# Two-block transformer kernel on one core: four TensorE products left out at the head of each of three attentions

## The chip, the cores and the metric

The kernel runs on one core of a Trainium2 chip. The metric is the device time of one execution, in microseconds (us); smaller is better. Three runs of the kernel before took 2171.41, 2173.5 and 2172.23 us.

## The reference

Two transformer blocks run one after the other over 512 tokens of width 1024, all in float32. What matters here are their three softmax attentions of 8 heads. Cut to what is computed:

```python
def first_block(x, ...):
    # o_a: 8 heads of 64; keys chosen by an index score, plus a relative bias
    logits = jnp.einsum('bqhd,bqkhd->bhqk', qb, k_sel) * A_HEAD_DIM ** -0.5 + bias   # dim 64
    p = jax.nn.softmax(jnp.where(valid, logits, -jnp.inf))
    o_a = jnp.einsum('bhqk,bqkhd->bqhd', p, v_sel)
    x = x + jnp.concatenate([o_a, o_b], axis=-1) @ w_out     # o_b: gated linear attention
    return x + hier_moe(rmsnorm(x, norm2_g), ...)            # 32 experts

def hybrid_mixer(h, ...):
    o_mla = causal_block_attention(q_mla, k_mla, v_mla, 1 / sqrt(96))                # dim 96
    o_fox = causal_block_attention(fq, fk, fv, 1 / sqrt(64), cum_log_f)              # dim 64 + 2
    merged = sigmoid(gate_a) * (o_mla @ w_o_mla) + sigmoid(gate_b) * (o_fox @ w_o_fox)
    return merged @ w_out

def second_block(x, ...):
    x = x + gate_m * hybrid_mixer(rms_norm(x) * (1 + scale_m) + shift_m, ...)
    x = x + gate_f * moe_ffn(...)                            # 64 experts and a shared one
    return rms_norm(x, g_final)
```

## The kernel before

The program is a list of stages (L2423 to L2426): setup, first norm, mixers, first attention, first output, first experts; then the second norm, latents, latent attention, fox attention, merge, second experts, final norm. Each stage is made of one or more blocks. In a block, each engine has its own list of instructions with waits on semaphores written out by hand, and a block ends with a barrier that all engines pass together. A stage's loads are issued by SyncE inside its own blocks, and many of them wait for a count of products of TensorE.

The function `attention` (L902) is called three times: by `first_attention` (L1023, query and key of 64 rows, two heads packed on the upper and lower 64 rows, with a bias that GpSimd prepares at L1017 for up to six units ahead, and with rows of the other mixer gated on GpSimd between them at L1033 and L1036), by `latent_attention` (L2040, 96 rows) and by `fox_attention` (L2102, 66 rows). It works through 32 units, 8 heads times 4 tiles of 128 queries. Unit t of a head covers 128 (t + 1) keys. TensorE takes turns between the scores of unit i (L934: 64, 96 or 66 rows, 128 to 512 columns, bank i % 3), the transposes of the probabilities of unit i - 3 (L943: 128 rows, 128 columns, t + 1 of them, banks 3 and 4) and the output products of unit i - 5 (L953: 128 rows, 64 columns, t + 1 of them, banks 5 and 6). VectorE adds the mask or bias and takes the maximum (L990), negates it (L993), inverts the sum (L998) and scales the output (L1000). ScalarE takes the exponential (L972) and copies the transposes (L966).

At the head of TensorE's list stand four products (L926, L927; WARM_UP is 4 at L32): the identity times the causal mask, 128 rows, 512 columns, into bank 7. Attention writes banks 0 to 6 only, nothing waits for the four or reads bank 7, and they wait for nothing but the barrier.

What stands around the attentions: the mixers stage ahead of the first one ends with small products of TensorE (L579, L590) and work of VectorE and ScalarE (L740 to L827). `heads_to_columns` (L2008, transposes at L2021) stands ahead of the second and third. Behind the first come `turn_rows` (L1125: 32 transposes at L1138) and `add_rows_product` (L1163). Elsewhere the text speaks of these lines: L487 is the product of a helper in the mixers (the index scores on 32 rows among them, L487 also the projections on 128 rows), L507 and L508 are products with one output column, L339 are the transposes of a norm, L1360 is the router's product with 64 columns.

Of the kernel before, what the change touches and what calls it, by code (L numbers as in the profile page):

```python
# [28 lines left out]
TAKEN = -float(2 ** 120)  # L29
SENTINEL = float(2 ** 100)  # L30
NO_TOKEN = 4096
WARM_UP = 4  # L32
HEADS = 8
FE = 256
FH = 2
# [197 lines left out]
def product(K, mm):  # L233

    mm.then_inc(K.products, 1)
    K.n_products += 1
    return K.n_products
# [664 lines left out]
def attention(K, tag, dim, out_col, bias=None, keep=None, loads=(), heads=None, rest=None):  # L902

    nc = K.nc
    s = K.sem
    maxed, expd, turned = s(f"{tag}_max_ready"), s(f"{tag}_probs_ready"), s(f"{tag}_turned_copied")
    scored, normed = s(f"{tag}_logits_read"), s(f"{tag}_out_normed")  # L910
    query, key = heads or (lambda h: K.qt[0:dim, h, :], lambda h: K.kt[0:dim, h, :])
    z = K.scr[:, 3072:4608].rearrange("p (b s) -> p b s", b=3)
    RING = 6
    offsets = K.scr[:, 0:512 * RING].rearrange("p (b s) -> p b s", b=RING)
    offset_ready = s(f"{tag}_offsets_ready")
    probs = K.scr[:, 8192:10240].rearrange("p (b s) -> p b s", b=4)
    turn = K.scr[:, 4608:6144].rearrange("p (b s) -> p b s", b=3)
    mx, neg, rsum, rinv = (K.small[:, 576 + 32 * n:608 + 32 * n] for n in range(4))
    units = [(h, t) for h in range(HEADS) for t in range(T)]
    N = len(units)  # L920
    at_s, at_t, at_o = [], [], []
    with nc.Block(no_gpsimd_drain=True) as block:
        @block.tensor
        def _(pe):

            for _ in range(WARM_UP):  # L926
                pe.matmul(K.bank[7][:, :], K.ident[:, :], K.causal[:, :], start=True, stop=True)  # L927
            for i in range(N + 5):
                if i < N:
                    h, t = units[i]  # L930
                    n = P * (t + 1)
                    if i >= 3:
                        pe.wait_ge(scored, i - 2)
                    at_s.append(product(K, pe.matmul(K.bank[i % 3][:, 0:n], query(h)[:, P * t:P * t + P],  # L934
                                                     key(h)[:, 0:n], start=True, stop=True)))
                if 3 <= i < N + 3:
                    u = i - 3
                    h, t = units[u]
                    pe.wait_ge(expd, u + 1)
                    if u >= 2:  # L940
                        pe.wait_ge(turned, u - 1)
                    for k in range(t + 1):
                        mm = pe.transpose(K.bank[3 + u % 2][:, P * k:P * k + P], probs[:, u % 4, P * k:P * k + P],  # L943
                                          K.ident[:, :])
                    at_t.append(product(K, mm))
                if i >= 5:
                    u = i - 5
                    h, t = units[u]
                    pe.wait_ge(turned, u + 1)
                    if u >= 2:  # L950
                        pe.wait_ge(normed, u - 1)
                    for k in range(t + 1):
                        mm = pe.matmul(K.bank[5 + u % 2][:, 0:64], turn[:, u % 3, P * k:P * k + P],  # L953
                                       K.v[:, k, 64 * h:64 * h + 64], start=k == 0, stop=k == t)
                    at_o.append(product(K, mm))

        @block.scalar
        def _(act):
            for i in range(N + 3):
                if i >= 3:  # L960
                    u = i - 3
                    n = P * (units[u][1] + 1)
                    act.wait_ge(K.products, at_t[u])
                    if u >= 3:
                        act.wait_ge(K.products, at_o[u - 3])
                    act.activation(turn[:, u % 3, 0:n], K.bank[3 + u % 2][:, 0:n], ACT.Copy).then_inc(turned, 1)  # L966
                if i < N:
                    n = P * (units[i][1] + 1)
                    act.wait_ge(maxed, i + 1)
                    if i >= 4:  # L970
                        act.wait_ge(K.products, at_t[i - 4])
                    act.activation(probs[:, i % 4, 0:n], z[:, i % 3, 0:n], ACT.Exp, bias=neg[:, i:i + 1],  # L972
                                   accum_out=rsum[:, i:i + 1]).then_inc(expd, 1)

        @block.vector
        def _(dve):
            step = K.dve.on(dve)
            for i in range(N + 5):
                if i < N:
                    h, t = units[i]  # L980
                    n = P * (t + 1)
                    dve.wait_ge(K.products, at_s[i])
                    if i >= 3:
                        dve.wait_ge(expd, i - 2)
                    zi, logits = z[:, i % 3, 0:n], K.bank[i % 3][:, 0:n]
                    mask = K.causal[:, S - n:S]
                    if bias is not None:
                        dve.wait_ge(offset_ready, i + 1)
                        mask = offsets[:, i % RING, 0:n]
                    dve.tensor_tensor_reduce(zi, logits, mask, 1.0, float(MASKED) * 2, ALU.add, ALU.max,  # L990
                                             mx[:, i:i + 1]).then_inc(scored, 1)
                    dve.wait_ge(scored, i + 1)
                    dve.tensor_scalar(neg[:, i:i + 1], mx[:, i:i + 1], -1.0, None, ALU.mult).then_inc(maxed, 1)  # L993
                if i >= 5:
                    u = i - 5
                    h, t = units[u]
                    dve.wait_ge(expd, u + 1)
                    step(dve.reciprocal(rinv[:, u:u + 1], rsum[:, u:u + 1]))  # L998
                    dve.wait_ge(K.products, at_o[u])
                    dve.tensor_scalar(K.hr[:, t, out_col + 64 * h:out_col + 64 * h + 64], K.bank[5 + u % 2][:, 0:64],  # L1000
                                      rinv[:, u:u + 1], None, ALU.mult).then_inc(normed, 1)

        @block.sync
        def _(sp):
            for place, src, arrived in loads:
                sp.dma_start(place, src).then_inc(arrived, 16)

        @block.gpsimd
        def _(pool):
            if bias is None:  # L1010
                return
            pool.wait_ge(K.bias_in, 32)
            for i, (h, t) in enumerate(units):
                n = P * (t + 1)
                if i >= RING:
                    pool.wait_ge(scored, i - RING + 1)
                pool.tensor_tensor(offsets[:, i % RING, 0:n], bias(h)[:, S - n:S], keep[:, t, 0:n],  # L1017
                                   ALU.add).then_inc(offset_ready, 1)
                if rest and i % 4 == 3:
                    rest(pool, i // 4)  # L1020
# [1434 lines left out]
```

## Time and profile before

| what | us |
| --- | --- |
| median of three runs | 2172.23 |
| the profiled execution's own time | 2176.87 |
| its span, first to last instruction | 2175.1 |
| TensorE busy with matmuls | 1940.5 |
| VectorE busy | 1203.3 |
| ScalarE busy | 952.8 |
| GpSimd busy | 589.4 |

### The profile page before, as it was taken

Reading aid. Unit: us, or ns where it says so; the run is one execution under the profiler, and the core shown is the slowest. Engines: PE = TensorE matmul, PEld = TensorE weight load, DVE = VectorE, ACT = ScalarE, POOL = GpSimd, SP = SyncE. Lnnn points to the kernel's source line nnn. Section 1 sums busy time; section 2 is a strip of 40 time slices with the busy share of each in tenths; the row PEclk is TensorE's granted clock in tenths of the full one; section 3 lists DMA queues with packets and bytes.
Section 4 is the critical chain, followed back from the end, with each engine's and each line's share of the span. In section 5 each row is a group of like instructions: output and inputs, shape, how many; then the busy total and the mean of one; then the engine's idle time right before and its main releaser. Section 6 shows DMA issues by size and latency. Waiting matters only on the chain. (4 is left out here: it accounts for less than half of the span.)

```text
span 2175.1 us, 27110 instructions
## 1 busy us (share of the span) xinstructions
PE 1940.5 (89%) x8280; PEld 1332.8 (61%) x8280; DVE 1203.3 (55%) x2222; ACT 952.8 (44%) x1620; POOL 589.4 (27%) x435
## 2 busy tenths in 40 slices
PE   7989989976999997689998988979999999999992
PEld 3533435765777665367876876647766666666661
DVE  1755413526777774246164344447777777777663
ACT  2411214523666553356264222146655555555551
POOL 4799995101222222000000000012222222222221
PEclk9799989986999999789999999789999999999996
DMA  5353422351999994211202335229999999999983
GB/s 176 114 184 117 163 77 72 135 195 54 336 334 325 327 324 135 89 49 40 78 6 78 108 115 218 83 94 344 338 338 327 324 331 337 322 337 326 317 280 98
DMA packets 120530, 437.44 MB, mean 201 GB/s; under 512 B 31920, under 2 KB 36416, under 8 KB 83328
## 3 DMA queue, kind: packets, MB, share of 16 engines
q1 hardware_dynamic: 92760, 402.69, 50.2%
q0 software_dynamic: 27648, 33.67, 7.0%
q8 instruction: 45, 0.74, 0.1%
q14 instruction: 37, 0.30, 0.0%
q10 hardware_dynamic: 40, 0.05, 0.0%
HBM read 442.51 MB, written 63.48 MB: 233 GB/s over the span
## 5 line engine op out<-in xcount | busy, mean ns | idle before, releaser
L1528 DVE TENSOR_TENSOR big_parts<-big,h_cols_parts 128x1024 fp32r<-128x1024 f32 x384 | 460.1, 1222 | 126.9 <-ACT h_cols_parts L1581 118.4
L1581 ACT ACTIVATE h_cols_parts<-big 128x1024 fp32r<-128x1024 f32 x384 | 395.7, 1057 | 99.9 <-PE bank L1489 64.8
L1518 PE MATMUL bank<-big,heads 128*128 128x512 f32 x768 | 352.7, 602 | 1.5 <-ACT heads L1589 1.5
L1792 POOL DMA_INDIRECT acc_scratch<-heads,small x96 | 159.5, 1662 | 618.0 <-DVE small L1559 386.3
L1487 PE MATMUL bank<-h_cols_parts,heads_parts 128*128 128x512 f32 x768 | 312.7, 407 | 15.9 <-DVE heads_parts L1549 15.7
L1489 PE MATMUL bank<-h_cols_parts,heads_parts 128*128 128x512 f32 x768 | 304.0, 396 | 0.0
L1488 PE MATMUL bank<-big_parts,heads_parts 128*128 128x512 f32 x768 | 302.7, 394 | 0.0
L1518 PEld LDWEIGHTS bank<-big,heads 128*128 128x128 f32 x768 | 138.3, 190 | 139.8 <-issue 137.8
L1614 ACT ACTIVATE heads<-bank 128x512 f32<-128x512 f32 x96 | 57.4, 598 | 335.4 <-DMA acc_scratch<-heads,small 262.9
L1619 POOL MEMSET heads<- 128x2048 f32 x2 | 3.6, 1805 | 687.2 <-POOLq L1354 687.2
L1487 PEld LDWEIGHTS bank<-h_cols_parts,heads_parts 128*128 128x128 f32 x768 | 147.3, 192 | 47.7 <-DVE heads_parts L1549 11.3
L1489 PEld LDWEIGHTS bank<-h_cols_parts,heads_parts 128*128 128x128 f32 x768 | 146.2, 190 | 32.2
L1488 PEld LDWEIGHTS bank<-big_parts,heads_parts 128*128 128x128 f32 x768 | 146.9, 191 | 28.2
L487 PE MATMUL bank<-big,h_cols 128*128 128x512 f32 (+1 forms) x384 | 163.0, 580 | 0.0
L1631 POOL DMA_INDIRECT heads<-h_scratch,small x96 | 114.2, 1190 | 168.5 <-DVE small L1559 139.6
L1101 PE MATMUL bank<-big_parts,heads_parts 128*128 128x512 f32 x352 | 139.8, 397 | 0.0
L487 PEld LDWEIGHTS bank<-big,h_cols 128*128 128x128 f32 x384 | 73.2, 210 | 89.1 <-issue 88.5
L1549 DVE TENSOR_TENSOR heads_parts<-bank,heads_parts 128x512 fp32r<-128x512 f32 x192 | 123.1, 681 | 2.6 <-ACT heads_parts L1607 2.6
L1498 PE MATMUL bank<-ident,heads 128*128 128x128 f32 x768 | 105.8, 282 | 19.6 <-DMA heads<-h_scratch,small 19.0
L1498 PEld LDWEIGHTS bank<-ident,heads 128*128 128x128 f32 x768 | 98.8, 192 | 37.8 <-DMA heads<-h_scratch,small 32.7
L1607 ACT ACTIVATE heads_parts<-bank 128x512 fp32r<-128x512 f32 x192 | 103.7, 596 | 9.3 <-PE bank L1498 9.3
L1557 DVE TENSOR_SCALAR small<-bank 128x1 int32<-128x1 f32 x96 | 21.1, 219 | 141.9 <-DMA acc_scratch<-heads,small 140.3
(361 smaller groups left out, 3014.4 us busy)
## 6 DMA issues: line engine op xcount, KB each, us to landing
big<-in_w_exp_down_dram SPq DMA_DIRECT2D x96, 1024.0 KB, 14.2
big<-in_w_exp_gate_dram SPq DMA_DIRECT2D x96, 1024.0 KB, 7.1
big<-in_w_exp_up_dram SPq DMA_DIRECT2D x96, 1024.0 KB, 14.7
big<-in_w_in_dram SPq DMA_DIRECT2D x13, 2048.0 KB, 8.9
junk<-in_w_mod_dram SPq DMA_DIRECT2D x12, 1024.0 KB, 5.1
spare<-in_w_mod_dram SPq DMA_DIRECT2D x12, 1024.0 KB, 5.1
big<-in_w_out_dram SPq DMA_DIRECT2D x4, 2048.0 KB, 10.4
h_scratch<-h_rows SPq DMA_DIRECT2D x8, 512.0 KB, 7.6
```

What stands on the lines that cost most here:

```text
L487: mm = pe.matmul(out, lhsT, rhs, start=c == 0, stop=c == len(lhs_rhs) - 1)
L1101: pe.matmul(banks[t][:, :], a_high, low, start=False, stop=False)
L1487: pe.matmul(b_au[b][:, :], x_high, gu_high[:, :, c, :], start=c == 0, stop=False)
L1488: pe.matmul(b_au[b][:, :], x_high, gu_low[q][:, :, c, :], start=False, stop=False)
L1489: mm = pe.matmul(b_au[b][:, :], x_low, gu_high[:, :, c, :], start=False, stop=c == KC - 1)
L1498: mm = pe.transpose(b_xt[half][:, P * k:P * k + P], xg[:, b, 4 * half + k::KC], K.ident[:, :])
L1518: mm = pe.matmul(b_y[half][:, :], hidt[:, b, P * j:P * j + P], dn[q][:, j, 512 * half:512 * half + 512], start=j == 0, stop=j == FH - 1)
L1528: dve.tensor_tensor(gu_low[q][:, :, part, :], gu[q][:, :, part, :], gu_high[:, :, part, :].bitcast(F32), ALU.subtract).then_inc(w_low, 1)
L1549: dve.tensor_tensor(xt_low[:, b, part], b_xt[half][:, :], xt_high[:, b, part].bitcast(F32), ALU.subtract).then_inc(xt_low_ready, 1)
L1581: act.activation(gu_high[:, :, part, :], gu[q][:, :, part, :], ACT.Copy).then_inc(w_high, 1)
L1631: pool.indirect_dma_start(out=xg[:, b, :], out_offset=None, in_=K.h_dram, in_offset=bass.IndirectOffsetOnAxis(idx[:, q:q + 1], 0), bounds_ ...
L1792: return pool.indirect_dma_start(out=K.acc_dram, out_offset=bass.IndirectOffsetOnAxis(at, 0), in_=rows, in_offset=None, bounds_check=S - 1 ...
```

## The change

The loop of four products at the head of TensorE's list in `attention` is left out, and with it the constant. All three attentions are built by this function, so twelve products go. Nothing is put in their place.

```diff
@@ -29,7 +29,6 @@
 TAKEN = -float(2 ** 120)
 SENTINEL = float(2 ** 100)
 NO_TOKEN = 4096
-WARM_UP = 4
 HEADS = 8
 FE = 256
 FH = 2
@@ -922,9 +921,6 @@
     with nc.Block(no_gpsimd_drain=True) as block:
         @block.tensor
         def _(pe):
-
-            for _ in range(WARM_UP):
-                pe.matmul(K.bank[7][:, :], K.ident[:, :], K.causal[:, :], start=True, stop=True)
             for i in range(N + 5):
                 if i < N:
                     h, t = units[i]
```

## Rows read from the trace of the kernel before

**Rows 1.** Timeline of TensorE at the three heads: start us, us, instruction, idle before.

```profile
348.01 6.68 PE L927 MATMUL bank<-causal,ident 128*128 128x512 f32 x8 [4.15 <-PEq L469]
354.63 2.42 PE L934 MATMUL bank<-heads 64*128 64x128 f32 x8
...
965.59 3.67 PE L927 MATMUL bank<-causal,ident 128*128 128x512 f32 x8 [1.30 <-PEq L2013]
969.10 2.32 PE L934 MATMUL bank<-heads 96*128 96x128 f32 x8
...
1093.11 3.67 PE L927 MATMUL bank<-causal,ident 128*128 128x512 f32 x8 [1.33 <-PEq L2013]
```

**Rows 2.** Stretches: us, busy PE, PEld, DVE, ACT, POOL, PEclk, DMA, GB/s.

```profile
343.90:347.20 3.30, 0.00 (x0) 0.00 (x0) 1.48 (x4) 2.38 (x4) 0.00 (x0) 1.00 0.00 0
347.40:354.00 6.60, 5.99 (x7) 2.52 (x8) 0.02 (x1) 1.28 (x1) 5.44 (x7) 0.50 0.21 24
354.20:407.00 52.80, 52.80 (x306) 36.84 (x304) 31.95 (x159) 31.71 (x96) 30.58 (x33) 1.00 0.01 1
...
969.10:1013.40 44.30, 44.27 (x305) 36.35 (x303) 31.25 (x159) 31.19 (x96) 0.00 (x0) 1.00 0.01 2
```

**Rows 3.** Timeline of ScalarE at the head of the second attention.

```profile
965.54 1.28 ACT L972 ACT_TABLE_LOAD   x1 [1.06 <-PEq L2013]
970.04 0.40 ACT L972 ACTIVATE big<-big,small 128x128 f32<-128x128 f32 x1 [3.21 <-DVE small L993]
```

**Rows 4.** Timeline of TensorE, parts of one head of the first attention.

```profile
371.31 0.70 PE L934 MATMUL bank<-heads 64*128 64x256 f32 x2
371.94 0.55 PE L943 MATMUL bank<-ident,big 128*128 128x128 f32 x3
...
377.02 1.00 PE L953 MATMUL bank<-heads,big 128*128 128x64 f32 x8
377.96 0.70 PE L934 MATMUL bank<-heads 64*128 64x256 f32 x2
```

**Rows 5.** Stretches elsewhere at 0.50, and one behind a rise.

```profile
65.50:80.70 15.20, 15.10 (x44) 8.62 (x43) 12.12 (x17) 8.92 (x20) 9.44 (x7) 0.50 0.66 237
...
84.40:87.80 3.40, 3.40 (x4) 1.39 (x5) 3.12 (x5) 3.37 (x4) 3.15 (x2) 0.50 0.02 5
...
466.90:470.10 3.20, 3.16 (x15) 3.16 (x16) 3.09 (x6) 3.14 (x8) 0.00 (x0) 0.50 0.92 265
470.20:472.10 1.90, 1.90 (x18) 1.88 (x17) 0.86 (x1) 1.90 (x5) 0.00 (x0) 1.00 1.03 423
...
1369.00:1379.00 10.00, 10.00 (x49) 10.00 (x48) 0.00 (x0) 0.29 (x1) 0.00 (x0) 0.50 0.59 210
```

**Rows 6.** Timeline of TensorE: what it ran in those stretches.

```profile
65.45 15.32 PE L487 MATMUL bank<-heads 32*128 32x256 f32 x42
...
82.49 1.86 PE L508 MATMUL bank<-shift,ident 12*1 12x512 f32 x2
84.28 5.88 PE L487 MATMUL bank<-h_cols,big 128*128 128x512 f32 x9
...
466.94 5.33 PE L339 MATMUL bank<-ident,h_rows 128*128 128x128 f32 x32 [5.72 <-DVE h_rows L373]
...
1368.05 13.88 PE L1360 MATMUL bank<-small,h_cols 128*128 128x64 f32 x64 [1.13 <-PEq L329]
```

**Rows 7.** Timeline of the weight loads of the four products, first and third head.

```profile
349.00 0.34 PEld L927 LDWEIGHTS bank<-causal,ident 128*128 128x128 f32 x1 [0.52 <-issue]
349.85 0.34 PEld L927 LDWEIGHTS bank<-causal,ident 128*128 128x128 f32 x1 [0.52 <-issue]
...
1093.61 0.19 PEld L927 LDWEIGHTS bank<-causal,ident 128*128 128x128 f32 x1 [0.24 <-issue]
1094.04 0.19 PEld L927 LDWEIGHTS bank<-causal,ident 128*128 128x128 f32 x1 [0.24 <-issue]
```

**Rows 8.** Timeline of TensorE behind the first attention.

```profile
407.80 3.77 PE L1138 MATMUL bank<-ident,h_rows 128*128 128x128 f32 x32 [0.79 <-PEq L922]
```

## The prediction

> **What bounds the kernel now.** I read the timeline of TensorE at the head of each attention first [rows 1]. The four products (eight records, since an fp32 product leaves two) stand at three places, and each time the scores of the attention's first unit start right behind them: 348.01 to 354.63 us, which is 6.62 us, and 965.59 to 969.10, which is 3.51; the third (from 1093.11) has the same 3.67 us busy as the second. No semaphore of theirs is waited for, and nothing reads bank 7 before it is written again, so what follows them on TensorE waits for them by order alone.
>
> Next the view by stretches [rows 2]. During the first attention TensorE is busy 52.80 of 52.80 us, while VectorE has 31.95, ScalarE 31.71 and GpSimd 30.58; the second has 44.27 of 44.30. Each attention is bounded by TensorE's own stream. The stages are closed by barriers, so whatever an attention gains or loses passes to the end of the kernel: the weights of later stages are issued inside their own stages and move with them.
>
> The column PEclk of the same rows is what matters most. TensorE stands idle from 343.9, the granted clock falls from 1.00 (2.4 GHz) to 0.50 (1.2 GHz) after 347.2, all but the last of the first head's products run at 0.50, the clock is back at 1.00 by 354.2, and the whole attention runs at 1.00. This is why the same four products take 6.62 us there and 3.51 at the other two heads, where only 1.30 and 1.33 us of idle time stand before them [rows 1] and the clock is 1.00 on both sides.
>
> **What is removed.** Second and third head: 3.51 us each on the path. The first scores then have to load their weights unhidden, some 0.1 us, so I take 3.4 each, 6.8 in all. ScalarE's table load of 1.28 us from 965.54 [rows 3] then ends at 966.82; the first exponential, today at 970.04 [rows 3], moves up by those 3.5 us to about 966.5 and so waits 0.3 us more, while TensorE is still at its first four scores: it costs nothing. First head: 6.62 us on the path. Taken alone, that is 13.4 us, or 2158.8 from the median.
>
> **What the first attention loses.** With the products out, the attention meets the clock at 0.50. The question is whether its own work raises it. Look at what one head's worth of it is in steady state [rows 4]: scores on 64 rows (128, 256, 384 and 512 columns, two records each), transposes on 128 rows, and output products of 64 columns only, with weights loaded for each; 371.31 to 377.96 is one head of four units, 6.65 us. Full products of 512 columns stand nowhere in it on 128 rows.
>
> Now what TensorE did at 0.50 elsewhere [rows 5, 6]. From 65.5 to 80.7 us it was busy 15.10 of 15.20 with products on 32 rows (the index scores), and the clock stayed at 0.50. Products of one output column on 12 rows, from 82.49, take 1.86 us for two records, the pace of 0.50 too. Then 84.4 to 87.8, back-to-back products of 512 columns on 128 rows, ran at 0.50 and the clock rose right after: the nine records from 84.28 take 5.88 us, where nine at 0.50 take 7.7. From 1369 to 1379, with 128x64 products, the exact form of the attention's outputs, TensorE was busy 10.00 of 10.00 and the clock stayed at 0.50. Back-to-back 128x128 transposes did raise it (466.9 to 470.1 at 0.50, 470.2 on at 1.00). The attention is made of what did not raise it (thin rows, 64 columns) mixed with runs of at most four transposes. So I forecast that it starts at 0.50 and stays there to its end. That it held 1.00 in the run shown says only that it doesn't let the clock fall.
>
> The Trainium skill says otherwise at first sight: TensorE: Matmul & The Clock Gate, Part 1, gives the rule that TensorE's being busy releases the throttle. By that rule the attention would raise the clock itself, as in the first rival below. This trace disagrees with it if busy means instructions in flight, since the stretch from 1369 was wholly busy and stayed at 0.50. Part 4 of the same page says that transposes don't count as busy work for the clock; the trace disagrees there as well, by the rise at 470.1.
>
> **Its price.** At the two levels [rows 7]: weight loads of the four products' records, and so the records, come every 0.85 us at 0.50 (349.00, 349.85) and every 0.43 at 1.00 (1093.61, 1094.04), a factor of 1.99. Transposes: at 0.50, 15 in 3.2 us, 0.213 each [rows 5]; at 1.00, 32 in 3.77 less one latency of 0.28 [rows 8], 0.109 each: 1.95. 64-column products: 64 in 13.88 us, 0.217 each, at 0.50 [rows 6]; 8 in 1.00 less a latency of 0.27 [rows 4], about 0.11 at 1.00: about 1.95. At 1.00 one head takes 1280 columns of scores (2.5 times 512, each two records of 0.43: 2.15 us), 10 transposes (1.1) and 20 output records (2.2): 5.45 of its 6.65 us. The other 1.2 is the change between 64-row and 128-row weights, about 0.3 a unit. If that doesn't stretch, the head takes 5.45 x 1.95 + 1.2 = 11.8 us, a factor of 1.78; if all does, 1.99. Much of it is the load itself, which does scale, so I take 1.92. The attention runs from 354.63 to 407.01 (407.80 less the 0.79 idle [rows 8]), 52.4 us; at 0.50 it takes 93.3 to 104.3, taken as 100.6. It costs 48.2 us more and starts 6.6 earlier: +41.6 net, bounds +34.3 and +45.3. VectorE, ScalarE and GpSimd, with 32 us of work each, don't become a bound in 100.
>
> Behind it, the turning stage's 32 transposes [rows 8] begin at 0.50; they raise the clock as those at 466.9 did. At worst they take 6.8 instead of 3.4 us; ScalarE and VectorE copy beside them. I take +1.5, bounds 0 and +3.4. From there on all is as before.
>
> **Sum:** +41.6 - 6.8 + 1.5 = +36.3 us. The profiled execution has 2176.87 us (span 2175.1 and 1.8 around it), so 2213 for one like it; it stands 4.6 above the median of the runs shown. From the median 2172.23: 2208.5, I say 2208. Bounds of this case: 34.3 - 7.0 + 0 = +27.3 and 45.3 - 6.6 + 3.4 = +42.1, or 2199 to 2215.
>
> **Rivals.** (1) The attention raises the clock itself, about when the four products do now (354.1). For it: TensorE will be wholly busy from 348.0, and opens with four scores of 1280 columns in all; 64 rows are more than 32. Against it: the stretches of [rows 5]. At 354.1 some 6.1 us at 0.50 have done 3.2 us of the attention's work, so 2.9 are lost and 6.6 - 2.9 = 3.7 saved there, with 6.8 at the others: 10.5, or 2161.7. This is the case on the other side. Its point: each microsecond that the attention spends at 0.50 costs 0.48 (1 - 1/1.92), so 13.4 us saved are used up after 28 us at 0.50. Above that the change is slower, below it faster. Chance 0.09.
> (2) The clock rises part of the way through the first attention, in a stretch rich in transposes: from 2168 to 2199. Chance 0.05.
> (3) A second attention drops as well. The third starts, without the products, with 66-row scores right behind 1.33 us of idle time and transposes. If the clock falls there, its 44 us (the second has 44.3 [rows 2]) take 1.9 times as long: about +41 more, 2249. Against: with 96 and 66 rows these attentions hold 1.00 today, and the idle time is a third of the 4.15 before the first [rows 1]. Chance 0.05.
> (4) The clock isn't down when the first attention begins, so that the products simply vanish: 13.4 saved, 2158.8. It fell after 3.3 us of idle time that this change leaves as it is. Chance 0.01.
> That the products stay in the program by another way is excluded: they are issued nowhere else.
>
> **How the numbers follow.** The forecast has the remaining 0.80. Its own range, 2199 to 2215, with a margin of 2 for runs and for the clock's moments elsewhere, holds perhaps 0.76; the upper part of rival 2 brings it to 8 in 10, so the range is 2178 to 2217. A measurement of this kernel tells 0.2% (4.3 us) from no change. Faster by more than that: rivals 1 and 4 and a little of 2, 0.11. Within: 0.02. Slower: 0.87.
>
> **What would show it.** Right: PEclk 0.50 from about 347 to the end of the first attention, which lasts about 100 us, its score records at about twice today's mean, transposes every 0.21 us; second and third attention 44 us each at 1.00, starting directly after the barrier. Wrong: PEclk back at 1.00 by about 354 in the first attention and a length of some 55 us (rival 1); a third attention of 85 us (rival 3); or a first attention that is cold and takes under 90 us, which would say that the factor was taken too high.

## The result, and the profile after

The changed kernel takes 2244.22 us (median of 6 runs, 2239.94 to 2248.74), the kernel before 2172.27 in the same comparison (2171.41 to 2173.5): a ratio of 1.0333, interval 1.0319 to 1.0346. It is slower by 72 us, where +36 was forecast, and lies above the range. The profiled execution has 2243.65 us with a span of 2241.9; that of before had 2176.87 and 2175.1, so the two traces account for +66.8 of span; the rest of the +72 is that the profiled execution of before stands 4.6 us above its median and that of after 0.6 below.

The head of the page of the kernel after (busy times, and the rows of PE and of its granted clock in 40 slices):

```profile
span 2241.9 us, 27062 instructions
PE 2007.3 (90%) x8256; PEld 1388.8 (62%) x8256; DVE 1205.6 (54%) x2222; ACT 957.6 (43%) x1620; POOL 591.1 (26%) x435
PE   7989899985999999589998998779999999999992
PEclk9789895595999999689956999699999999999996
```

A slice is 56 us. In slices 7 and 8, which hold the first attention, TensorE is granted half speed: forecast. In slices 21 and 22 the clock is low a second time: that is the third attention, and it was not forecast. The other low slices have their like in the kernel before. Now the stretches of the kernel after, beside [rows 2]: us, busy PE, PEld, DVE, ACT, POOL with instructions, PEclk, DMA share, GB/s.

```profile
340.40:343.60 3.20, 0.28 (x3) 0.04 (x1) 1.45 (x3) 2.35 (x3) 0.00 (x0) 1.00 0.00 0
343.80:441.10 97.30, 96.27 (x304) 66.03 (x304) 32.19 (x160) 33.95 (x98) 35.99 (x40) 0.50 0.02 2
441.20:446.10 4.90, 4.19 (x20) 4.22 (x21) 2.36 (x4) 2.29 (x4) 0.00 (x0) 0.50 0.00 0
1003.10:1047.40 44.30, 44.30 (x304) 36.42 (x304) 31.26 (x159) 32.31 (x97) 0.00 (x0) 1.00 0.01 2
1118.00:1128.70 10.70, 8.69 (x71) 8.16 (x72) 6.47 (x14) 5.39 (x11) 0.00 (x0) 1.00 0.05 13
1128.90:1207.20 78.30, 78.30 (x282) 62.45 (x281) 30.01 (x149) 31.24 (x94) 0.00 (x0) 0.50 0.01 2
```

The granted clock falls at 343.7 us, at the end of the same idle time as before, and rises only at 446.1, some 4 us into the transposes that follow the first attention. The second attention runs at 1.00 throughout. The third begins at 1.00 and loses the clock at 1128.8, 1.6 us after its first product, and has it back at 1207.3, two microseconds before its end. VectorE and ScalarE have nearly the same work in each attention as before, only spread over a longer time. The timeline of TensorE of the kernel after at the same places as [rows 1, 4, 8] (start, us, instruction, idle time before it):

```profile
344.83 4.60 PE L930 MATMUL bank<-heads 64*128 64x128 f32 x8 [4.15 <-PEq L468]
...
441.91 5.76 PE L1134 MATMUL bank<-ident,h_rows 128*128 128x128 f32 x32 [0.79 <-PEq L921]
...
1003.10 2.40 PE L930 MATMUL bank<-heads 96*128 96x128 f32 x8 [1.30 <-PEq L2009]
...
1127.16 3.02 PE L930 MATMUL bank<-heads 66*128 66x128 f32 x8 [1.33 <-PEq L2009]
...
1203.47 1.81 PE L949 MATMUL bank<-heads,big 128*128 128x64 f32 x8
```

The first scores follow the idle time directly. In the first attention they start at 0.50 (4.60 us for eight records, 2.42 before [rows 1]). In the third they start at 1.00 and are overtaken by the fall (3.02 against the second's 2.40), and its output products late in the stage still take 1.81 for eight, where [rows 4] show 1.00 for the same eight at full clock.

By stage, first product to last, head included before:

| stretch | before | after | difference |
|---|---|---|---|
| up to the first head | 348.01 | 344.83 | -3.2 |
| first attention | 59.0 | 96.3 | +37.3 |
| between first and second | 558.6 | 562.0 | +3.4 |
| second attention | 47.8 | 44.3 | -3.4 |
| between second and third | 79.7 | 79.7 | 0 |
| third attention | 47.8 | 82.1 | +34.3 |
| after the third | 1034.2 | 1032.7 | -1.5 |

The sum is +66.9. The third attention alone is half of the loss. The stretches between move by 3.4 us or less here. In the profiled executions of the kernels below they move by as much or more: the first head starts at 343.0 to 349.4 us, the first and second attention stand 556.0 to 563.1 apart, and 1027.7 to 1035.6 follow the third. They are not read as effects.

### The profile page after: what moved, and what is told of

Its sections match the earlier page's. It is cut to its first block and busy times, and to the rows that moved or that the text cites. A ratio compares the mean times of both kernels' runs of the same rounds, so it can differ in the third digit from the quotient of the medians.

```text
span 2241.9 us, 27062 instructions
## 1 busy us (share of the span) xinstructions
PE 2007.3 (90%) x8256; PEld 1388.8 (62%) x8256; DVE 1205.6 (54%) x2222; ACT 957.6 (43%) x1620; POOL 591.1 (26%) x435
## 5 line engine op out<-in xcount | busy, mean ns | idle before, releaser
L930 PE MATMUL bank<-heads 64*128 64x128 f32 (+5 forms) x192 | 109.6, 675 | 6.8 <-PEq L468 4.1
```

## Experiments

The kernels ran in four groups, each group on one chip beside the kernel before: the four of the first part below, the four of the second part, then idle_again, idle_two and idle_first, and last head_first. The median of the kernel before was 2175.3, 2174.6, 2174.4 and 2174.8 us there, so kernels of different groups are best compared by their ratios. Each trace is of one execution.

### Which attention pays what

Three kernels start from the one before and give each attention its own number of products; only the dictionary differs:

```
-WARM_UP = 4
+WARM_UP = {"attn1": 4, "mla": 0, "fox": 0}    # first_only
+WARM_UP = {"attn1": 0, "mla": 0, "fox": 4}    # third_only
+WARM_UP = {"attn1": 4, "mla": 0, "fox": 4}    # first_third
-            for _ in range(WARM_UP):
+            for _ in range(WARM_UP[tag]):
```

A fourth starts from the changed kernel and puts products where TensorE stands idle anyway, ahead of the barrier: four behind the last work of the stage before the first attention, one behind the transposes that prepare the third, held until the bank that it writes has been copied out.

```
                 if c < 7:
                     mod_sum(loop_bank())
+            for _ in range(4):
+                pe.matmul(K.bank[0][:, :], K.ident[:, :], K.causal[:, :], start=True, stop=True)
...
+            fill = {"mla_turn": 0, "fox_turn": 1}[tag]
+            if fill:
+                pe.wait_ge(taken[0], 5)
+            for _ in range(fill):
+                pe.matmul(K.bank[0][:, :], K.ident[:, :], K.causal[:, :], start=True, stop=True)
```

> The four products stay at the head of the first attention alone. Both theories: first attention as before (59.0 us from the head on, clock 1.00 behind the products), second 3.4 us shorter. Theory A (the third attention cannot keep the clock at its head by itself: 66-row scores right behind 1.3 us of idle time): the third falls to 0.50 again and takes about 82 us, 2172.3 - 3.4 + 34.3 = 2203. Rival B (the third fell only because the slow first attention had moved it to another moment): it stays at 1.00, 2172.3 - 6.9 = 2165.

> The four products stay at the head of the third attention alone. Theory A: first attention at 0.50 throughout, 96 us instead of 59.0 (+37.3), some 3 us more behind it, second 3.4 shorter, third as before: 2172.3 + 37.3 + 3 - 3.4 = 2209. Rival C (once low, the clock of this program also costs the third): the third is slow in spite of its products, 2243.

> The four products stay at the first and the third attention, and go at the second alone. Theory A: only the second changes, its head of 3.5 us goes and it stays at 1.00: 2172.3 - 3.4 = 2168.9, slightly faster than the kernel before. Rival: the second, moved or bare, loses the clock in some executions, 2168.9 or about 2210 from run to run.

> No product at any head of an attention. Four products stand instead at the end of the mixers' TensorE list, ahead of the barrier where TensorE is idle for 4.15 us, and one at the end of the transposes ahead of the third attention (1.33 us idle). Theory A: the clock never falls ahead of the first or the third, and nothing on the path is added: 2172.3 - 6.6 - 3.4 - 3.4 = 2159. Rival D (one product is too little for the third): first fast, third at 0.50: 2159 + 38 = 2197. Rival E (four products that end 0.7 us ahead of the barrier don't hold the clock through a first attention that begins with 64-row scores): first at 0.50, 2200 or more.

Measured: first_only 2206.25 (4 runs, ratio 1.015, interval 1.0113 to 1.0186), third_only 2208.88 (4 runs, 1.0168, 1.0131 to 1.0206), first_third 2171.14 (12 runs, 0.9993, 0.9973 to 1.0013), idle_filled 2163.39 (12 runs, 0.9942, 0.9925 to 0.996). The stretches, first of first_only (its first attention; the end of the stage that prepares the third and the third itself, up to where its clock falls and behind it), then of third_only (first and third attention):

```profile
354.80:407.10 52.30, 52.30 (x304) 36.76 (x304) 31.99 (x159) 31.73 (x96) 30.75 (x34) 1.00 0.00 1
1082.00:1092.10 10.10, 7.71 (x67) 7.05 (x65) 5.50 (x8) 5.87 (x10) 0.00 (x0) 1.00 0.01 2
1092.20:1093.60 1.40, 1.40 (x7) 1.08 (x8) 0.84 (x6) 0.38 (x2) 0.00 (x0) 1.00 0.28 41
1094.00:1172.20 78.20, 78.20 (x282) 62.44 (x281) 29.95 (x149) 31.16 (x94) 0.00 (x0) 0.50 0.01 2
```

```profile
346.90:443.00 96.10, 96.10 (x304) 65.84 (x304) 31.96 (x159) 33.58 (x97) 35.81 (x40) 0.50 0.02 2
1132.70:1176.90 44.20, 44.20 (x305) 36.33 (x303) 31.30 (x159) 31.22 (x96) 0.00 (x0) 1.00 0.00 1
```

With the first attention left as it was, the third still loses its clock, 1.6 us after it begins, and takes 82.1 us; with the third's products kept, it does not, though the first is at 0.50 all along. Each loss comes without the other; first_only is 1.5% slower than the kernel before and third_only 1.7%, both with the 3.4 us of the second attention saved. The second attention's products carry nothing: first_third leaves them out, and the attention runs its 44.34 us at 1.00, as it does in every trace here that leaves them out. Its ratio can't be told from no change, though 3.4 us less (0.16%) would be expected; that is below what 12 runs tell.

Of idle_filled, the timeline of TensorE around the two fills, then the stretches of the first and third attention:

```profile
342.62 3.70 PE L620 MATMUL bank<-causal,ident 128*128 128x512 f32 x8
346.84 2.39 PE L932 MATMUL bank<-heads 64*128 64x128 f32 x8 [0.52 <-PEq L468]
...
1083.33 1.02 PE L2025 MATMUL bank<-causal,ident 128*128 128x512 f32 x2
1084.82 2.40 PE L932 MATMUL bank<-heads 66*128 66x128 f32 x8 [0.47 <-PEq L2011]
```

```profile
346.90:399.30 52.40, 52.29 (x304) 36.74 (x304) 31.97 (x159) 33.05 (x97) 35.70 (x40) 1.00 0.03 4
...
1084.80:1129.10 44.30, 44.28 (x304) 36.44 (x304) 31.28 (x159) 31.22 (x96) 0.00 (x0) 1.00 0.02 7
```

The idle time ahead of the first scores shrinks from 4.15 us to 0.52, that ahead of the third's from 1.33 to 0.47, and the clock is 1.00 on both sides of each. The products themselves run at 1.00 now (eight records in 3.70 us, 6.68 before [rows 1]), because the clock has not fallen where they stand. The median lies 12 us below the kernel before, where 13 were expected.

### Why an attention can't raise the clock, and why the third loses it

rows128 keeps everything of the changed kernel but lets the first attention's scores take 128 rows of weights and data instead of 64, in as many products of as many columns; the two heads of a pair are then summed in each score, so its output is not that of the kernel. moment puts two products ahead of the transposes that prepare the third attention; fox96 and fox66_same both clear rows 64 to 95 of the third's heads on GpSimd (the copies wait for it), and differ only in the rows that the scores read.

```
-    pair = lambda a: lambda h: a[64 * (h % 2):64 * (h % 2) + 64, h // 2, :]
+    pair = lambda a: lambda h: a[:, h // 2, :]                               # rows128
...
+            for _ in range(2 if tag == "fox_turn" else 0):                   # moment
+                pe.matmul(K.bank[0][:, :], K.ident[:, :], K.causal[:, :], start=True, stop=True)
...
+                    pool.memset(K.heads[64:96, 4096 * n:4096 * n + 4096], 0.0).then_inc(blank, 1)
-    attention(K, "fox", 66, 512,
+    attention(K, "fox", 96, 512,                                             # fox96; 66 in fox66_same
```

> The changed kernel, but the first attention's scores are taken on 128 rows (both heads of a pair at once), as many products of as many columns as before. Their values are the sums of two heads' logits, so this part of the computation is another one. Theory A (thin rows are why the first attention cannot raise the clock): the clock starts at 0.50 and rises within some 7 us, the attention takes 58 us or less instead of 96, third still at 0.50: 2244 - 38 = 2206 or less. Rival F (the 64-column output products or the number of idle moments are why): it stays at 0.50 to its end, 2240 or so.

> The changed kernel with two of the products put at the start of the transposes ahead of the third attention, so that everything after moves by 1.7 us and the 1.33 us of idle time with the 66-row scores behind it is as it was. Theory B2 (the third loses the clock by the moment at which that idle time comes, which is the same in every execution because it stands 73.4 to 73.5 us behind a rise of the clock in all traces so far): another moment, the clock stays, third 44.3 us, 2244 + 1.7 - 38 = 2208. Theory A (the sequence alone decides): the third falls again, 2246.

> The changed kernel with the third attention's scores on 96 rows, 30 of them zeros that GpSimd writes ahead of the copies (same output; the stage ahead gets up to 3 us longer). Theory A (rows): as the second attention, it keeps 1.00 and takes 44.3 us: 2244 + 3 - 38 = 2209. Rival: rows play no part at the head, third at 0.50, 2247.

> The control for the kernel with 96 rows: the same zeros and the same waits, but the scores on 66 rows. Theory A: third at 0.50, about 82 us, 2247. If it keeps 1.00 (2209), the move by 3 us alone decides and the run with 96 rows says nothing of rows.

Measured: rows128 2187.4 (3 runs, 1.0067, 1.0034 to 1.01), and with 2 runs each moment 2207.5 (1.0148, 1.0116 to 1.018), fox96 2208.97 (1.0154, 1.0107 to 1.0202), fox66_same 2246.87 (1.0329, 1.0299 to 1.0359). Stretches of rows128, from the idle time ahead of the first attention to its end:

```profile
343.00:346.30 3.30, 0.00 (x0) 0.00 (x0) 1.14 (x3) 2.22 (x3) 0.00 (x0) 1.00 0.00 0
346.60:349.90 3.30, 3.30 (x8) 1.98 (x8) 1.76 (x9) 2.11 (x6) 3.30 (x5) 0.50 0.43 47
350.20:392.30 42.10, 42.09 (x297) 35.05 (x295) 29.74 (x150) 29.95 (x92) 31.71 (x36) 1.00 0.01 2
```

The idle time is the same 4.15 us. The clock falls 0.2 us behind the first score and is back after 3.4 us, while the opening scores run. The same list with scores on 64 rows has it back nowhere among its scores; in moment, whose first attention is unchanged, the fall comes at nearly the same place, 0.4 us behind the first score, and the clock stays at 0.50 for 92 us. TensorE is wholly busy in all of them. So it is the rows of the opening scores that decide here, not idle time. Whether the 64-column outputs help to hold the clock down later on this does not tell, since none of them runs before the rise in rows128.

The whole attention takes 46.0 us, 6.4 less than the 52.4 before, 3.4 us of it at half clock. So some 8 us (52.4 less 44.4, an estimate for 46.0 without its half clock) belong to the 64-row scores, which the prediction put at 1.2 us a head, 9.6 for eight, as the change between 64-row and 128-row weights. It is not the change of rows as such: with 66-row and 96-row scores the same list takes 44.3 us. What it is in the 64-row scores no run here shows. The third attention of rows128 still takes 82.1 us, which is why the kernel stays slower than the one before.

The third attention of fox96 (its preparing stage, the part at 0.50, the rest), that of fox66_same, and the timeline of TensorE at the head of each, fox96 first:

```profile
1120.00:1132.60 12.60, 8.89 (x71) 7.78 (x69) 4.96 (x8) 6.03 (x12) 6.97 (x2) 1.00 0.00 1
1132.90:1139.40 6.50, 6.50 (x17) 4.29 (x18) 3.12 (x16) 3.16 (x11) 0.00 (x0) 0.50 0.15 40
1139.70:1180.20 40.50, 40.50 (x287) 33.90 (x285) 27.93 (x144) 28.19 (x85) 0.00 (x0) 1.00 0.01 1
```

```profile
1132.80:1214.50 81.70, 81.70 (x300) 65.14 (x298) 31.13 (x156) 31.93 (x94) 0.00 (x0) 0.51 0.00 1
```

```profile
1132.75 4.61 PE L930 MATMUL bank<-heads 96*128 96x128 f32 x8 [2.21 <-PEq L2010]
...
1130.83 4.60 PE L930 MATMUL bank<-heads 66*128 66x128 f32 x8 [2.21 <-PEq L2010]
```

In both the clock falls right at the attention's start, also with 96 rows, which the expectation had not looked for: clearing the rows lengthens the idle time ahead of the scores from 1.33 to 2.21 us, in the two kernels alike, so this pair does not test what the 96 rows do against the fall at 1.33. That the time of fox96 lands on the expected 2209 is therefore in part luck: its third attention takes 47.5 us and not 44.3. What the pair tells is the rise. With 96 rows the clock is back 6.8 us after the fall; with 66 rows only after 81.9, in the last 2 us of the attention. Until the rise the two run the same list at the same pace (4.61 and 4.60 us for the eight opening records), so a denser stream is not the reason. The attentions take 47.5 and 83.8 us, and the medians differ by 38, from 30 more rows of zeros.

The rises in the other traces fit this. In the kernel after, first_only, rows128 and fox66_same the third attention gets its clock back 5.1 to 5.6 us behind its last score, while only transposes and 64-column outputs are left, both on 128 rows. In moment the first attention does so too (last score to 436.0 us, rise at 441.8). In the other four kernels whose first attention is at 0.50 the same 9 us without scores don't raise it, and it comes back 5 to 6 us behind the attention, in the transposes; why it does so at one place and not at the other is not shown.

Timeline of TensorE of moment, ahead of the third attention:

```profile
1117.91 1.95 PE L2013 MATMUL bank<-causal,ident 128*128 128x512 f32 x4 [1.16 <-PEq L2057]
1119.70 7.15 PE L2019 MATMUL bank<-ident,big 128*66 128x128 f32 x64
1128.18 2.40 PE L930 MATMUL bank<-heads 66*128 66x128 f32 x8 [1.33 <-PEq L2009]
```

Here the idle time right ahead of the third's scores is still 1.33 us and the scores still have 66 rows, but two products stand 10 us earlier, and the clock does not fall: the attention takes 44.3 us. Both executions have the time that goes with it (2209.89 and 2205.12). So idle time ahead of thin scores is not enough by itself; where the head stands and what ran shortly before it count too. Which of the two it was here, the 1.8 us of work or the shift that it makes, one kernel can't tell. In fox66_same the third head stands 75.1 us behind the last rise of the clock, nearly as far as in moment (75.4; 73.4 to 73.6 in the others read below), and the clock falls all the same, but behind 2.21 us of idle time.

### The better version

Two sizes and two placings of the fill were compared. idle_two runs two products ahead of the third instead of one; idle_first fills ahead of the first and keeps the old four at the head of the third; head_first keeps the old four at the head of the first, has none at the second, and fills ahead of the third; idle_again is idle_filled once more.

> The same kernel as idle_filled once more, beside its two variants: 12 us below the kernel before, and now and then an execution some 37 us longer, as the one of 2200.53 among twelve. If no execution is longer this time, that one was not the kernel's.

> Two products instead of one at the end of the transposes ahead of the third attention. Theory A: the second product sticks out of the 1.33 us of idle time by about 0.4 us, no execution is 37 us longer: 12 us below the kernel before, or 11.5. Rival (the longer execution lost its clock elsewhere): it shows up here as well.

> Four products in the idle time ahead of the first attention, none at the second, the old four at the head of the third. Theory A: 6.6 + 3.4 = 10 us below the kernel before less nothing, so 3.5 above the kernel with one product ahead of the third, and no longer execution.

> The four products stay at the head of the first attention, none stand at the second, one stands in the idle time ahead of the third. Theory A: 3.4 + 3.4 = 7 us below the kernel before. On the rare executions that were 35 to 43 us longer with the products in the idle time ahead of the first attention (one of twelve, none of six, one of eight, one of twelve): if the first attention lost its clock in them, none shows up here; if the third did, one may.

| kernel | median, us | lowest and highest | runs | ratio (interval) |
|---|---|---|---|---|
| idle_filled | 2163.39 | 2153.52, 2200.53 | 12 | 0.9942 (0.9925 to 0.996) |
| idle_again | 2156.67 | 2153.86, 2157.70 | 6 | 0.9916 (0.9892 to 0.9939) |
| idle_two | 2163.11 | 2153.93, 2197.96 | 8 | 0.9941 (0.9916 to 0.9965) |
| idle_first | 2166.99 | 2160.72, 2209.58 | 12 | 0.9966 (0.9944 to 0.9988) |
| head_first | 2168.37 | 2160.12, 2171.94 | 12 | 0.9964 (0.995 to 0.9978) |

All five beat both kernels. Filling both idle times is worth 0.6 to 0.8%, 11 to 18 us; filling only one about 0.35%. All of these include the 3.4 us of the second attention. A second product ahead of the third adds 0.8 us of path (80.56 instead of 79.73 between the second and the third attention) and shows no gain: the intervals of idle_two and idle_again overlap. In 4 of 38 executions of the kernels that fill ahead of the first attention the time was 2198 to 2210, 34 to 43 us above the medians of their kernels: one each of idle_filled and idle_two, two of idle_first. The ratios leave these four out; spread over the 38 they take about 4 us of the gain away. Their mean granted clock is 0.906 to 0.912, against 0.925 to 0.932 in the other 34, which makes some 70 to 100 us more at half speed by an estimate from clock and span, about the length of one attention. The loss of the first attention costs 43.9 us and that of the third 37.8, and the times tell the two apart badly. In idle_first, though, the third has the four products that kept its clock in all 16 executions of third_only and first_third. That the fill ahead of the first attention now and then comes out too short would fit, but no trace caught such an execution, and it stays open. head_first had none in 12, which chance alone would give about one time in four at a rate of 4 in 38.

## Why the prediction was right and wrong

**Right: the first attention.** It starts at 0.50 and can't raise the clock: 96.3 us at 0.50, and the transposes behind it raise it, as [rows 5, 6] had them. Rivals 1 and 2 are out. Of the reasons that were read from the stretches elsewhere, rows128 and the pair fox96 and fox66_same show one, thin rows. The other, the 64-column outputs, no run tests by itself; against it stand the ends of the attentions, where the clock came back in five traces while only such outputs and transposes ran. The Trainium skill's rule (TensorE: Matmul & The Clock Gate, Part 1, that the engine's being busy releases the throttle) fails here in its plain form: 96.27 us busy of 97.30 and a PEclk of 0.50. The rule in Part 4 of the same page of the Trainium skill, that transposes don't count as busy work for the clock, gets no support either: nothing but 4.2 us of transposes ran between the attention and the rise at 446.1. This case is weaker than that of [rows 5, 6], since the end of the attention, without scores, stands right ahead of it.

**A term mis-sized: the factor.** Taken as 1.92, bounds 1.78 to 1.99; measured 96.3 / 52.4 = 1.84. So the term is +37.3 where +41.6 stood, 4 us too much. What was off is the part that doesn't scale, not the factor of the products. The third attention shows this: 78.5 us of it at 0.50 do what takes 40.7 at 1.00 (44.3 less the 3.6 at 1.00), a factor of 1.93, near the 1.95 of the prediction; its whole ratio, 82.1 / 44.3 = 1.85, is a mixture of both clocks. With 1.93 on 44.3 of the 52.4 us, 10.8 of the first attention's 96.3 are left for the 8.1 us that only the 64-row scores have, an estimate of 1.3 for that part, which the price took nearly as if it stretched with the rest.

**Right: second attention, and what stands behind the first.** -3.44 us, taken as 3.4. The product that follows the turning stage's transposes starts 9.6 us after them instead of 8.3 (+1.35, taken as 1.5). In the whole stretch up to the second attention this can't be seen: 562.0 us here, 558.6 before, 556.0 to 563.1 in the others.

**Wrong: the third attention.** The failed step is rival 3, with a chance of 0.05. It named the place (66-row scores right behind 1.33 us of idle time), the mechanism and a price of +41, 2249; measured were +34.3 for that attention instead of the -3.4 of the sum, and 2244. The sum held that this attention keeps its clock without the products; it doesn't. What argued it away was "with 96 and 66 rows these attentions hold 1.00 today, and the idle time is a third of the 4.15 before the first". Both are true and neither bears on it. The kernel before holds 1.00 there with the four products standing on that very spot: first_only and first_third, which differ in the third's products alone, show that it was the products that held it. And the idle time was compared with that of the first head, although the trace had no case of idle time with scores right behind it, at any head; moment shows that even the same 1.33 us may or may not do it.

Nor is the loss a matter of chance. TensorE bounds the stage ahead of the third attention, and the distance from the clock's rise in front of that stage to the third head hardly moves: 73.4 us in the kernel before (1019.7 to 1093.11), 73.5 in the one after (1053.7 to 1127.16) and in first_only (1018.7 to 1092.20), 73.6 in rows128 (998.5 to 1072.17). In the last three, which have no products there, the fall comes 1.5 to 1.6 us behind the head. The six runs of the kernel after lie within 0.4% of each other: no execution of it kept the clock.

**What follows for the sum.** Had the third been taken as rival 3 has it, at the +34.3 that it measured, and the factor at 1.84, the sum would have been +37.3 + 1.5 - 3.4 + 34.3 = +69.7, against +66.8 between the traces and +72 between the medians.

## What to carry to other kernels

Before products that nothing reads are taken out, ask at each place separately whether they hold the clock there, and don't take "the clock is at 1.00 there today" for an answer, because today they are there: what the stage behind them could do alone can only be read from its own products. Here attentions with 64-row or 66-row scores did not raise the clock as long as scores ran, and one of them did not keep it behind 1.33 us of idle time. At half clock the first cost 1.84 times its length, and the cold part of the third 1.93 times, so a product or two is cheap insurance; but it belongs in the idle time ahead of the barrier and not behind it, where it is paid for in full and, as at the first head, at half speed. Then look at many executions: with the fill ahead of the first attention, 4 in 38 were still some 40 us longer.

## What was not expected of the hardware

With scores on 64 or 66 rows the clock stayed at 0.50 through 92 to 96 and 78 to 82 us of unbroken work; with scores on 96 rows it was back 6.8 us after its fall, on 128 rows after 3.4. Yet the same 64-row attention, begun at 1.00, ran its 52.4 us at 1.00 each time (before, first_only, first_third and the kernels that fill): what work keeps the clock and what work brings it back are not the same. And with two products of 1.8 us that ended 8 us ahead of the third attention its clock stayed, with the idle time in front of it unchanged.
